# VectorE's order in the token-shift mixer: the first power's copy, a half reciprocal, the key norms and four convolutions

## What is computed

```
us = u + (previous row of u - u) * mu
r, k, v, w_low, a_low, g_low = split(us)
decay = exp(-exp(-softplus(-(w0 + tanh(w_low) @ w2)) - 0.5))
a     = sigmoid(a0 + a_low @ a2)
gate  = sigmoid(g_low) @ g2
kk    = k * k_k;  kk = kk * rsqrt(max(sum over a head of kk*kk, 1e-24))     # the key norms
k     = k * (1 + (a - 1) * k_a)
for each token:  s = s * decay + (s @ -kk) (kk*a)^T + v k^T;   y = s @ r
y = ((y - mean) * rsqrt(var + 64e-5)) * ln_g + ln_b + (sum r*k*r_k) * v;  y = y * gate
xbc = conv(xbc, 4 taps, causal, each column by itself) + bias               # third mixer
```

## Time and profile before

| | us |
|---|---|
| median of three executions | 1475.73 |
| lowest and highest | 1473.58, 1477.09 |
| the profiled execution | 1474.93 |
| its span (first to last instruction) | 1473.2 |
| TensorE busy in the span | 1435.6 |
| VectorE busy | 719.7 |
| ScalarE busy | 409.0 |
| GpSimd busy | 220.1 |

### The profile page before, as it was taken

How to read it: one execution, slowest core, us unless ns; L and a number is a source line. 1 busy time by engine, 2 the same in 40 slices (tenths; PEclk the granted TensorE clock), 3 DMA queues, 4 the chain that set the end, 5 groups by cost and what they waited for, 6 DMA issues and landing times.

```text
span 1473.2 us, 32470 instructions
## 1 busy us (share of the span) xinstructions
PE 1435.6 (97%) x13605; PEld 1047.9 (71%) x13605; DVE 719.7 (49%) x1359; ACT 409.0 (28%) x842; POOL 220.1 (15%) x182
## 2 busy tenths in 40 slices
PE   7999999999999999999999999999999999999997
PEld 6999677677777777777769976775576766667652
DVE  7442878877655677734557663522212112112116
ACT  2333444343422544435432111111111111111111
POOL 3784103130110000020022000001010000000000
PEclk9999999999999999999999999999999999999999
DMA  7896473754244544565577548599999999999994
GB/s 282 186 194 155 124 211 100 204 171 131 75 127 143 135 119 114 181 196 177 153 257 184 213 165 356 191 395 417 427 426 428 428 427 428 427 429 427 428 376 186
DMA packets 157474, 375.41 MB, mean 255 GB/s; under 512 B 102150, under 2 KB 110742, under 8 KB 139664
## 3 DMA queue, kind: packets, MB, share of 16 engines
q1 hardware_dynamic: 141648, 346.64, 66.3%
q0 software_dynamic: 7008, 16.50, 3.2%
q10 hardware_dynamic: 8672, 10.20, 2.0%
HBM read 328.72 MB, written 51.95 MB: 258 GB/s over the span
## 4 chain that ended last, share of the span: by engine, by line
PE 87%; DMA 5%; DVE 4%; ACT 1%; DVEq 1%; issue 1%; ACTq 0%; SPq 0%
PE PS L718 23%; PE PS L1284 14%; PE PS L735 7%; PE PS L1303 7%; PE PS L1251 6%; PE PS L1130 5%; PE PS L802 4%; DMA region<-moe_w 3%; PE PS L1111 2%; PE PS L1172 2%; PE PS L1256 2%; DVE region L1787 1%; PE PS L810 1%; DMA region<-wo 1%; PE PS L1267 1%
## 5 line engine op out<-in xcount | busy, mean ns | idle before, releaser
L718 PE MATMUL PS<-h0T,region 128*128 128x320 f32 x1360 | 389.0, 438 | 1.7 <-issue 1.5
L1412 ACT ACTIVATE region<-PS 128x320 f32<-128x320 f32 (+5 forms) x350 | 144.9, 425 | 684.1 <-PE PS L718 232.3
L718 PEld LDWEIGHTS PS<-h0T,region 128*128 128x128 f32 x1360 | 252.0, 190 | 110.0 <-issue 13.0
L1284 PE MATMUL PS<-region 128*64 128x512 f32 x1024 | 229.2, 593 | 0.5 <-DMA region<-moe_w 0.5
L1284 PEld LDWEIGHTS PS<-region 128*64 128x64 f32 x1024 | 128.2, 137 | 87.6 <-issue 23.5
L1787 DVE TENSOR_TENSOR region<-region 128x512 f32<-128x512 f32 (+10 forms) x232 | 157.1, 697 | 32.6 <-DMA region<-wo 6.7
L1412 ACT ACTIVATE region<-region 128x256 f32<-128x256 f32 (+10 forms) x228 | 99.3, 466 | 119.8 <-DVEq L2207 24.5
L1303 PE MATMUL PS<-region,history 128*64 128x512 f32 x512 | 119.4, 597 | 1.0 <-ACTq L1745 0.5
L1787 DVE TENSOR_TENSOR history<-region,PS 128x256 f32<-128x256 f32 x32 | 13.5, 421 | 217.5 <-ACTq L1740 217.5
L1412 ACT ACT_TABLE_LOAD x77 | 98.8, 1283 | 26.3 <-ACTq L1459 9.5
L1794 DVE SCALAR_TENSOR_TENSOR region<-region,feature_vectors 128x320 f32<-128x320 f32 (+1 forms) x103 | 76.8, 745 | 56.1 <-ACTq L1488 41.0
(11 more groups left out here) (247 smaller groups left out, 1613.9 us busy)
## 6 DMA issues: line engine op xcount, KB each, us to landing
region<-moe_w SPq DMA_DIRECT2D x64, 2048.0 KB, 28.3
region<-moe_w SPq DMA_DIRECT2D x64, 1024.0 KB, 26.3
region<-w_in SPq DMA_DIRECT2D x115, 512.0 KB, 5.6
region<-wo SPq DMA_DIRECT2D x32, 512.0 KB, 4.5
expert_rows<-region SPq DMA_DIRECT2D x20, 512.0 KB, 6.9
region<-expert_rows SPq DMA_DIRECT2D x5, 2048.0 KB, 21.7
projected<-region ACTq DMA_DIRECT2D x59, 167.5 KB, 3.6
region<-projected SPq DMA_DIRECT2D x10, 768.0 KB, 6.5
```

Source lines behind the costliest of these rows:

```text
L718: last = mm(PS[:, 6 + i % 2, 0:NTOK], WR[:, i, k, :], H0T[:, k, :], start=(k == 0), stop=(k == KT - 1))
L1284: last = mm(PS[tiles(i), 2, :], XE[:, k, tiles(i)], W13[r][i][:, k * 512:k * 512 + 512], start=(k == 0), stop=(k == KT - 1))
L1412: return nc.scalar.activation(out, in_, f, **kw)
```

## The change

On VectorE:

- In chunks 1 to 4 the first half of the late reciprocal (late_root(0)) stands behind the copy of the first power instead of ahead of it.
- In chunk 0, convolve(33) moves from ahead of the whole chunk to behind the copy of the first power, convolve(34) from ahead of the masks to the same place (behind 33), and convolve(35) from there into turn 0 of the rounds.
- The convolutions of the chunk's own first three tiles stand in turns 0, 1 and 2 instead of 0, 2 and 3.
- front_norms stands in turn 3 instead of 4, front_sums in turn 4 instead of 3.

On TensorE the product of the key norms stands behind round 2 and its fill instead of behind round 3 and its half fill. ScalarE's, GpSimd's and SyncE's lists stay as they are; no operation is added or removed.

```diff
--- before.py
+++ after.py
@@ -908,7 +908,7 @@
                         fill(5, first)
                     if r == 4:
                         fill(*((4, first) if six else (5, second)))
-                    if r == 3 and ahead:
+                    if r == 2 and ahead:
                         front_norms(c + 1)
                     if r == 3:
 
@@ -2001,8 +2001,6 @@
                 if late:
                     convolve(STARTS[c] - 2)
                     late_variance(c - 1)
-                else:
-                    convolve(N_RW - 2)
                 dve.wait_ge(sem("rw_scores"), c * 3 + 1)
                 for k2 in range(2):
                     tt(SB[:, 4 * k2:4 * k2 + 4].rearrange("p a b c -> p a (b c)"),
@@ -2018,16 +2016,16 @@
                 for h in range(2):
                     tt(head(PTT, 1 - h)[:, 4:8, 1, :], head(SB, h)[:, 4:8, 0, :], head(E, h).unsqueeze(1).to_broadcast([64, 4, L]), add)
                 dve.drain().then_inc(sem("rw_lv"), 1)
-                if late:
-                    late_root(0)
                 dve.wait_ge(sem("rw_scores"), c * 3 + 3)
                 w = banks(0, 2, 8, 2, L)
                 dve.tensor_copy(in_two(PSK[:, 0]), pair(4))
                 dve.drain().then_inc(sem("rw_psk"), 1)
-                if c > 0:
+                if late:
+                    late_root(0)
                     convolve(STARTS[c] - 1)
                 else:
-                    convolve(N_RW - 1)
+                    convolve(PRE + 1)
+                    convolve(N_RW - 2)
                 for rd in range(5):
                     i = (rd + 1) % 2
                     dve.wait_ge(sem("rw_power"), c * 5 + (rd + 1))
@@ -2040,16 +2038,16 @@
                     if rd == 0 and late:
                         late_root(1)
                         dve.drain().then_inc(sem("rw_varc"), 1)
-                    if rd == 0:
-                        convolve(STARTS[c])
-                    elif rd in (2, 3):
-                        convolve(STARTS[c] + rd - 1)
+                    if rd == 0 and not late:
+                        convolve(N_RW - 1)
                     if rd == 1 and ahead:
                         front_rates(c + 1)
+                    if rd < 3:
+                        convolve(STARTS[c] + rd)
                     if rd == 3 and ahead:
+                        front_norms(c + 1)
+                    if rd == 4 and ahead:
                         front_sums(c + 1)
-                    if rd == 4 and ahead:
-                        front_norms(c + 1)
                 dve.wait_ge(sem("rw_inverse"), c * 6 + 6)
                 dve.tensor_copy(TT, w[:, :, 1])
                 dve.drain().then_inc(sem("rw_tt"), 1)
@@ -2093,7 +2091,6 @@
             front_norms(0)
             front_sums(0)
             front_keys(0)
-            convolve(PRE + 1)
             rwkv(0, False, True)
             for c in range(1, NPC):
                 rwkv(c, True, True)
```

## The result

| | before | changed |
|---|---|---|
| median of seven runs each, us | 1475.39 | 1486.53 |
| lowest, highest | 1472.85, 1479.35 | 1477.44, 1488.76 |
| profiled execution | 1474.93 | 1477.44 |
| its span | 1473.2 | 1475.6 |

The ratio is 1.007, interval 1.0053 to 1.0088: slower, by 11 us of medians. 2.4 us more had been forecast, up to 1482. The profiled execution is the fastest of the seven and the only one near the forecast, so its trace shows the mechanism, and not the whole price. One execution of one later kernel (c0_clears_spread, 2465.44 us at a mean granted clock of 0.558) was a slow one and is left out of its ratio and its columns.

The account below looks back on a forecast made before the run. TensorE, busy 97% of the span, was taken as the bound. Chunk 0 +2.7, chunks 1 and 2 -2.2 and +0.1, chunk 3 +1.8 sum to +2.4 us: 1478.1 us on the median of 1475.73, range 1474.0 to 1482.0.

Parts of the forecast that it names:

- chunk 0, round 0 starts sooner: Chunk 0, TensorE: waits for the operands (1.19 us) and first power (1.11) shrink or go; round 0 starts 2.2 us sooner.
- landing of tile 33's store: Chunk 0: GpSimd's store of tile 33 was taken to land in 4.2 us; ScalarE's move of tile 37 waits for it.
- idle before L823: Chunk 0: TensorE idles 5 us for the turned keys before the low-rank products; chunk 0 is 2.7 us later in all.
- chunks 1 and 2, wait before round 0: Chunks 1 and 2: TensorE's waits for the first power, 1.14 and 1.04 us, go; 2.2 us won.
- chunk 3, wait before round 5: Chunk 3: TensorE waits 2.1 us for VectorE, held by the reciprocal of the earlier key norms; net 1.8 us lost.
- waits before round 5 in chunks 0 to 2: Chunks 0 to 2: VectorE's work for the earlier key norms is just hidden, with 0.1 to 0.4 us to spare.
- Carrying shifts to the end one for one: Behind chunk 4: every shift reaches the end in full, as fills, later phases and weights' transfers follow TensorE's progress.
- a phase to 450 us that isn't 2 to 3 us longer: Sign of being wrong: the whole phase from 165 to 450 us is not 2 to 3 us longer.
- The gaps that end on 'issue': TensorE's idle gaps in the middle of runs of equal matmuls, 1.53 us in chunk 1, taken to stay unchanged.
- Rival (e): TensorE's issue gaps, 0.3 to 1.5 us a chunk, fall elsewhere: +-1.5 us on every case; no chance given.
- Each us of landing is a us: Chunk 0: its delay follows the landing of tile 33's store one for one: 3.6 gives 2.1 us, 5.6 gives 4.1.
- (a): Chunk 0: tile 33's store lands after 4.8 us or more, ending the same wait later: 1479 to 1484 us; chance 0.25.

Follow-up runs that it names:

- c0_clears_spread: Kernel before with only chunk 0's three convolutions moved as in the change, and the stores of zeros spread one per fill; ratio 1.0009.
- norms_alone: Kernel before with only the key norms one round sooner on TensorE and VectorE, a convolution still ahead of them in turn 3; ratio 1.0046.
- after_again: The changed kernel as it is, timed once more; ratio 1.008, profiled execution 1483.18 us.
- c0_alone: Kernel before with only chunk 0's three convolutions moved as in the change; ratio 1.0026.
- root_alone: Kernel before with only the half reciprocal moved behind the first power's copy in chunks 1 to 4; ratio 0.9981.
- root_clears_spread: Kernel before with the half reciprocal behind the first power's copy, and the stores of zeros spread one per fill over chunks 0 to 2; ratio 0.9966.
- conv33_root_clears_spread: Changed kernel with tile 33's convolution between operands and masks, key norms in their old place, and the stores of zeros spread one per fill; ratio 0.9963.
- conv33_root: Changed kernel with chunk 0's convolution of tile 33 between operands and masks, and the key norms back in their old place; ratio 1.0014.
- clears_spread: Kernel before with only SyncE's stores of zeros spread one per fill over chunks 0 to 2; ratio 0.9983.
- c0_undone: Changed kernel with chunk 0's convolutions of tiles 33, 34 and 35 back in their old places; ratio 1.0048.

## Why the prediction was wrong

Its rows for the change's own waits held:

| step | forecast | after |
|---|---|---|
| chunk 0, round 0 starts sooner | 2.2 us | 1.19 and 1.11 gone, 0.17 left |
| landing of tile 33's store | 4.2 | 4.14 |
| idle before L823 | 5 | 4.74 |
| chunks 1 and 2, wait before round 0 | gone | gone |
| chunk 3, wait before round 5 | 2.1 | 1.98 |
| chunk 3, old wait of 0.28 | gone | gone |
| waits before round 5 in chunks 0 to 2 | none | none |

Waits that end on another engine fell by 4.76 us (1.19, 1.11, 1.14, 1.04, 0.28) and grew by 6.89 (0.17, 4.74, 1.98): +2.1, for +2.4. Carrying shifts to the end one for one held too: from the end of the mixer to the end of the span lie 1022.8 us in before, 1021.8 in the changed kernel and 1023.4 in norms_alone. What it left out is larger than what it summed.

That the profiled execution took 1477.44 us, for 1477.3 in the sum, is luck. Its mixer is 4.8 us longer than in before (303.1 against 298.3), not 2.4; the prediction had named just this, a phase to 450 us that isn't 2 to 3 us longer, as a sign of being wrong. But it began at 150.62 instead of 152.10, though the two kernels are the same up to there (after_again began at 152.30), and the rest of the execution behind it was 1.0 us shorter.

**First failed step: "The gaps that end on 'issue' ... wait for no semaphore of the change, and I leave them as they are."** That they wait for no semaphore is true, and the conclusion isn't. They grew from 3.4 us to 5.5 in the profiled execution and 7.4 in that of after_again, because TensorE now comes to the dense stretch with less time behind it, while its next packet of instructions waits for DMA engines that SyncE's stores, and the load of rows behind them, keep full. Rival (e) had them as a symmetric ±1.5 on every case. They were a term of 2 to 4 us with a sign: an edit which takes time out of TensorE's list ahead of such a stretch can hand it to the stall.

**Second failed step: "Each us of landing is a us".** An idle time of 4.74 us costs more than itself. Its price behind it is 0.83 us on L823 (1.99 for 1.16) and 0.58 on the half fill (3.00 for 2.42), 1.4 us in this trace; in c0_alone the clock column grows by about 2 us, and over the changed kernel's runs by 5 to 5.6 (8.5 against 2.9 to 3.6). The Trainium skill (TensorE: Matmul & The Clock Gate, "Part 1: The HAM clock gate") says that an idle TensorE is put back to half its clock pulses. This trace agrees (0.77, 0.50, 0.50, 0.52 from the last of the 4.74 us on). The prediction forecast 5 us of idle time and read the clock in the profile of before, 1.00, as if it were a constant.

In order of size for 11 to 12 us: about 5 of clock (an estimate, and part of it behind the stalls), 2 to 4 of stalls, 2.1 of the waits that were summed, 9 to 11 in all. Of the rivals, (a) named slower, but its cause, a late landing, was not it: the landing came when forecast.

The version that beats both kernels is root_alone (0.9981), and further root_clears_spread (0.9966), which takes from the change only the half reciprocal behind the first power's copy; conv33_root_clears_spread (0.9963) can't be told from it.

## What to carry to other kernels

When a bound engine shows idle time that nothing in the profile releases, find out what it shares with its neighbours before calling it fixed: count the engine's instructions up to each such place, as they here came out at one place in every 256, put the DMA share beside it, and move the transfers as an experiment. Before a part is undone because it cost time, check that it wasn't a shorter path into such a stall: here the same edit (conv33_root) was worth +2.1 us with the bursts and -3.0 against clears_spread without. And price an idle time of some us on TensorE at itself plus the slow stretch behind it.

## What the runs showed of the hardware

- The granted clock also fell behind a stall of 2.37 us that no semaphore explains. norms_alone, stretches of 4 us:

```profile
207.00:211.00 4.00, 3.71 (x51) 2.74 (x51) 3.52 (x4) 2.49 (x4) 0.00 (x0) 0.69 1.34 226
211.00:215.00 4.00, 3.81 (x99) 2.85 (x97) 1.38 (x2) 3.75 (x8) 0.00 (x0) 0.89 0.86 229
```

  It did not behind the one of 2.11 us in the changed kernel's profile (1.00 from 272 to 280 us), nor behind 2.60 us in c0_undone (1.00 from 272 to 284), but it did behind 1.30 us in root_alone (0.50 from 273.2 on). So in these traces the length of the stall alone doesn't tell. The seven runs of the changed kernel lie within 11.4 us, the five of root_clears_spread within 3.4.
- Twenty stores of 512 KB off every path, moved from three bursts to one a fill (and with them the load of rows behind each burst), gave 2.5 us on the kernel before and 2.2 more on root_alone's.
- Instructions took 2.07 MB of DMA traffic, 0.6% of the engines' time, and still TensorE stood up to 3.00 us, always at one place in each 256 of them.
